# Layer norm in column halves, the key tiles earlier in the weight stream, and two query tiles split by token tile

## What is computed

```python
merged = (sigmoid(gate_fox) * (y_fox @ p_fox) + sigmoid(gate_rwkv) * (y_rwkv @ p_rwkv))
x = layer_norm(DN_ALPHA * x + merged @ w_o, ln1_g, ln1_b)
x = layer_norm(DN_ALPHA * x + peer(x, w_q, sub_keys, u_table, v_table), ln2_g, ln2_b)

def layer_norm(x, g, b):
    mu = mean(x); var = mean((x - mu) ** 2)
    return (x - mu) * rsqrt(var + 1e-5) * g + b

# peer, per token: q = x @ w_q as 8 heads x 2 halves of 128; scores against 128 keys per list;
# the top 16 of each of the 16 lists, the top 16 of their 256 sums, softmax gates,
# h = gelu(u_table[idx] @ x), output = (gate * h) @ v_table[idx]
```

## Time and profile before

| | |
|---|---|
| median of 3 runs | 1415.6 us (1414.64 to 1416.53) |
| the profiled execution, its own time | 1418.0 us |
| its span in the profile | 1416.3 us |
| TensorE busy | 1382.9 us, 98% of the span |
| VectorE, ScalarE, GpSimd busy | 892.2, 869.3, 764.5 us |
| mean granted TensorE clock | 0.994 |

### The profile page before, as it was taken

The page is one execution under the profiler, slowest core; times in us unless marked ns, Lnnn a source line. Parts: engine busy times, 40 slices in busy tenths (PEclk is TensorE's granted clock), DMA queues, the critical chain, the costliest instruction groups (busy, mean ns, idle before and its releaser), DMA issues.

```text
span 1416.3 us, 28596 instructions
## 1 busy us (share of the span) xinstructions
PE 1382.9 (98%) x9422; PEld 1220.7 (86%) x9422; DVE 892.2 (63%) x1967; ACT 869.3 (61%) x1496; POOL 764.5 (54%) x350
## 2 busy tenths in 40 slices
PE   7999999999999999999999999999999999999997
PEld 6878888887888777789999999999998888888886
DVE  3784883214753654435998049999977776655555
ACT  5475775446755656556666768888874544444443
POOL 6876889877765523877988877777750000000000
PEclk9999999999999999999999999999999999999999
DMA  6633566555443312654555556566559877666662
GB/s 199 209 124 119 193 194 194 185 185 166 147 149 122 127 53 75 208 187 155 193 178 188 180 175 201 190 201 198 200 189 329 273 243 240 208 193 191 194 193 96
DMA packets 75352, 256.63 MB, mean 181 GB/s; under 512 B 8472, under 2 KB 8856, under 8 KB 75032
## 3 DMA queue, kind: packets, MB, share of 16 engines
q1 hardware_dynamic: 64192, 231.76, 50.2%
q10 hardware_dynamic: 11096, 24.00, 4.9%
HBM read 244.72 MB, written 11.01 MB: 181 GB/s over the span
## 4 chain that ended last, share of the span: by engine, by line
PE 70%; POOL 12%; issue 8%; DVE 6%; ACT 2%; DMA 0%; POOLq 0%; ACTq 0%; DVEq 0%
PE PS L1079 60%; POOL WL L403 12%; PE PS L1124 2%; PE PS L1637 2%; PE PS L1458 1%; PE PS L1125 1%; PE PS L1416 0%; DVE GA L1804 0%; DMA fbias<-fox_bias 0%; PE PS L1363 0%; DVE H L1994 0%; DVE XS L2270 0%; DVE GA L1803 0%; DVE BK L2008 0%; PE PS L1613 0%
## 5 line engine op out<-in xcount | busy, mean ns | idle before, releaser
L403 POOL TENSOR_TENSOR WL<-RAW,WH 128x1024 fp32r<-128x1024 f32 x306 | 740.2, 2429 | 278.6 <-ACT WH L462 190.8
L1079 PE MATMUL PS<-XHL,WH 128*128 128x256 f32 x2528 | 460.8, 284 | 2.2 <-DVE XHL L1757 1.5
L953 ACT CAST WH<-RAW 128x1024 fp32r<-128x1024 f32 x252 | 263.6, 1046 | 226.5 <-PE PS L1079 211.6
L1079 PEld LDWEIGHTS PS<-XHL,WH 128*128 128x128 f32 x2528 | 394.5, 192 | 5.8 <-issue 4.0
L1079 PE MATMUL PS<-XHL,WL 128*128 128x256 f32 x1264 | 357.8, 283 | 0.0
L462 ACT CAST WH<-RAW 128x1024 fp32r<-128x1024 f32 x184 | 191.3, 1047 | 109.4 <-PE PS L1079 98.7
L1079 PEld LDWEIGHTS PS<-XHL,WL 128*128 128x128 f32 x1264 | 242.7, 192 | 0.0
L2440 DVE TENSOR_TENSOR WL<-RAW,WH 128x1024 fp32r<-128x1024 f32 x128 | 156.8, 1225 | 120.2 <-ACT WH L953 119.5
L1079 PE MATMUL PS<-WH,CH 128*128 128x512 f32 x512 | 199.2, 389 | 0.0
L1079 PE MATMUL PS<-WH,CL 128*128 128x512 f32 x512 | 199.2, 389 | 0.0
L1079 PE MATMUL PS<-WL,CH 128*128 128x512 f32 x512 | 199.2, 389 | 0.0
(11 more groups left out here) (407 smaller groups left out, 1966.4 us busy)
## 6 DMA issues: line engine op xcount, KB each, us to landing
RAW<-weights SPq DMA_DIRECT2D x438, 512.0 KB, 3.6
gates_rest<-stage ACTq DMA_DIRECT2D x32, 272.0 KB, 2.2
stage<-gates_rest ACTq DMA_DIRECT2D x32, 272.0 KB, 4.1
H<-x SPq DMA_DIRECT2D x2, 512.0 KB, 4.8
LG<-rows ACTq DMA_DIRECT2D x2, 512.0 KB, 6.3
LB<-rows ACTq DMA_DIRECT2D x2, 512.0 KB, 8.8
x<-H ACTq DMA_DIRECT2D x1, 1024.0 KB, 5.8
HY<-x ACTq DMA_DIRECT2D x1, 1024.0 KB, 13.4
```

The lines of the kernel that those rows point to most:

```text
L403: nc.gpsimd.tensor_tensor(WL[:, slot, :], RAW[:, slot, :], plain(WH[:, slot, :]), ALU.subtract).then_inc(w_lo, 1)
L953: nc.scalar.copy(WH[:, slot, :], RAW[:, slot, :]).then_inc(w_hi, 1)
L1079: last = mm(dst, a, b, start=start and k == 0, stop=stop and k == len(pairs) - 1)
```

## The change

Three edits:
1. `keys` moves in the item order from behind `w_o` to ahead of `p_rwkv`. `KK` gets another address; `fox_item(3)` counts `w_used` up by 3 in place of the keys (before, the last `w_o` item did). The places of `feed` from `p_fox` to `p_rwkv` stay as they are.
2. The layer norm works in column halves. Sums stay in PSUM; ScalarE squares each half around a pivot (twice the mean of half 0, with sign), and one-column operations of VectorE put the variance together. Half 0 of a tile is summed when its half of the product is complete (`tile_done`, `w_used`). Gain and shift are applied half by half.
3. TensorE transposes tile 0 ahead of the last `w_o` item of tile 1, multiplies `peer_q` 0 and 1 with tile 0, transposes tile 1, and multiplies the two with tile 1; `tile_low(0)` stands in VectorE's program between the two halves of tile 1. The last `v_table` items are split by halves for tile 1 alone.

```diff
-    ... ("p_fox", 4), ("p_rwkv", 4), ("w_o", 8), ("keys", 2), ("peer_q", 16), ...
+    ... ("p_fox", 4), ("keys", 2), ("p_rwkv", 4), ("w_o", 8), ("peer_q", 16), ...
-        KK = at("KK", [P, 2, 2, D], F32R, R0 + 16384)
+        KK = at("KK", [P, 2, 2, D], F32R, A0 + 40960)

 # ScalarE
-            act.wait_ge(w_used, FIRST["p_rwkv"])
+            act.wait_ge(w_used, FIRST["keys"])
...
-            feed(FIRST["w_o"] + 6)
+            feed(FIRST["w_o"] + 4)
+            def row_squares(k, t, half):
+                c = 2 * k + t
+                act.wait_ge(sem("mean_ready"), 2 * c + half + 1)
+                A(LNS[:, t, half * 512:(half + 1) * 512], PS[:, row_bank(k, t, half), :], ACT.Square,
+                  bias=row_stat(c, PIVOT), accum_out=row_stat(c, SQUARES + half)).then_inc(sem("var_ready"), 1)
+            def row_root(k, t, ms_val):
+                r = ST[:, 96 + 2 * k + t:97 + 2 * k + t]
+                act.wait_ge(sem("ms_ready"), ms_val)
+                A(r, r, ACT.Sqrt, scale=-1.0 / D ** 2).then_inc(sem("sq_ready"), 1)
+            root_table()
+            row_squares(0, 0, 0)
+            row_squares(0, 0, 1)
+            row_root(0, 0, 9)
+            feed(FIRST["w_o"] + 5)
+            feed(FIRST["w_o"] + 6)
+            tile_high(0, range(4))
+            row_squares(0, 1, 0)
+            row_squares(0, 1, 1)
+            row_root(0, 1, 10)
+            feed(FIRST["w_o"] + 7)
+            tile_high(1, range(2))
+            feed(FIRST["peer_q"])
+            tile_high(1, range(2, 4))

 # TensorE
-                last.then_inc(w_used, 1)
+                last.then_inc(w_used, 3 if c == 3 else 1)          # fox_item
             for t in range(NT):
                 for j in range(4, 8):
                     g, i = W_O_ORDER[j] // 4, W_O_ORDER[j] % 4
                     activations(T_MERGED)(2 * i + 1)
+                    if (t, j) == (1, 7):
+                        tile_transposes(0)
                     last = item_a(FIRST["w_o"] + j, i, XH, XL, 2 * g, False, i == 3, [t])
                     if t == NT - 1:
-                        last.then_inc(w_used, 1 if j < 7 else 3)
-                if t == 0:
-                    last.then_inc(sem("tile_done"), 1)
+                        last.then_inc(w_used, 1)
+                    elif j % 2:
+                        last.then_inc(sem("tile_done"), 1)
+            def query_tile(m, t):
+                ...
+                for k in range(KC):
+                    if m == 0:
+                        wait("xl_ready", KC * T_X2 + 4 * t + k // 2 + 1)
+                    mm(both[:, :, tokens], wh, XHL[:, :, k, tokens], start=(k == 0), stop=False)
+                    last = mm(both[:, 0, tokens], wl, XH[:, k, tokens], start=False, stop=(k == KC - 1))
-            for m in range(LISTS):
+            for t in range(NT):
+                if t:
+                    tile_transposes(t)
+                for m in range(2):
+                    query_tile(m, t)
+            list_scores(0)
+            for m in range(2, LISTS):
                 wait("ql_ready", m - 3)
-                item_w(FIRST["peer_q"] + m, 4 + m % 4, ready=...)
-                if m:
-                    list_scores(m - 1)
+                item_w(FIRST["peer_q"] + m, 4 + m % 4)
+                list_scores(m - 1)
 # last v_table items
-            for t in range(NT):
+            for c in range(4):
+                last = v_item(NK - 4 + c, c, stop=(c == 3), tiles=[0])
+            last.then_inc(sem("tile_done"), 2)
+            for half in range(2):
                 for c in range(4):
-                    last = v_item(NK - 4 + c, c, stop=(c == 3), tiles=[t])
+                    last = v_item(NK - 4 + c, c, stop=(c == 3), tiles=[1], halves=[half])
                 last.then_inc(sem("tile_done"), 1)

 # VectorE
+            def first_half(k, t, alpha):
+                link(V.scalar_tensor_tensor(rows, (HY if k else H)[:, t, halves[0]], alpha, rows, ALU.mult, ALU.add,
+                                            accum_out=sums))
+                V.tensor_scalar(row_stat(c, PIVOT), sums, -2.0 / D, None, ALU.mult).then_inc(sem("mean_ready"), 1)
+            def second_half(k, t, alpha, gain, shift, landed, ready, beside=None):
+                V.scalar_tensor_tensor(rows[1], H_[:, t, halves[1]], alpha, rows[1], ALU.mult, ALU.add,
+                                       accum_out=sums[1]).then_inc(sem("mean_ready"), 1)
+                wait("mean_ready", 2 * c + 2)
+                V.tensor_scalar(m, sums[0], sums[1], -1.0 / D, ALU.add, ALU.mult)
+                V.tensor_scalar(apart, sums[1], sums[0], None, ALU.subtract)
+                wait("var_ready", 2 * c + 1)
+                link(V.tensor_scalar(rest, row_stat(c, SQUARES), float(D), LN_EPS * D * D, ALU.mult, ALU.add))
+                link(V.scalar_tensor_tensor(spread, apart, apart, rest, ALU.mult, ALU.subtract))
+                wait("var_ready", 2 * c + 2)
+                V.scalar_tensor_tensor(r, row_stat(c, SQUARES + 1), -float(D), spread, ALU.mult, ALU.add).then_inc(
+                    sem("ms_ready"), 1)
+                wait("ln_landed", landed)
+                V.scalar_tensor_tensor(rows[0], rows[0], m, gain[:, halves[0]], ALU.add, ALU.mult)
+                if beside:
+                    beside()
+                wait("sq_ready", 9 + c)
+                link(V.reciprocal(r, r))
+                V.scalar_tensor_tensor(H_[:, t, halves[0]], rows[0], r, shift[:, halves[0]], ALU.mult,
+                                       ALU.add).then_inc(sem(ready), 1)
+                link(V.scalar_tensor_tensor(rows[1], rows[1], m, gain[:, halves[1]], ALU.add, ALU.mult))
+                V.scalar_tensor_tensor(H_[:, t, halves[1]], rows[1], r, shift[:, halves[1]], ALU.mult,
+                                       ALU.add).then_inc(sem(ready), 1)
             for t in range(NT):
+                alpha = ST[:, 104 + t:105 + t]
                 if t == 0:
                     wait("tile_done", 1)
                 else:
+                    used(FIRST["w_o"] + 5)
+                first_half(0, t, alpha)
+                if t == 0:
+                    wait("tile_done", 2)
+                else:
+                    tile_low(0)
                     used(FIRST["w_o"] + 7)
-                layer_norm(0, t, [t, 2 + t], ST[:, 104 + t:105 + t], LG1, LB1, 32, "x2_ready")
-            tile_low(0)
+                second_half(0, t, alpha, LG1, LB1, 32, "x2_ready")
             tile_low(1)
 # the second norm: first_half(1, 0); second_half(1, 0) with first_half(1, 1) behind its first gain pass
 # (beside); second_half(1, 1), which waits for tile_done 6
```

More of the change, by code:

```diff
@@ L61 @@
     ("qk", 8), ("v", 8), ("o", 8), ("mix_out", 8), ("w1", 32), ("w2", 32), ("ple", 2), ("ple_gate", 8),
-    ("rwkv", RW_CHUNKS), ("fox_qk", 8), ("fox_v", 4), ("gates", 16), ("p_fox", 4), ("p_rwkv", 4), ("w_o", 8),
-    ("keys", 2), ("peer_q", 16), ("u", NK), ("v_table", NK),
+    ("rwkv", RW_CHUNKS), ("fox_qk", 8), ("fox_v", 4), ("gates", 16), ("p_fox", 4), ("keys", 2), ("p_rwkv", 4),
+    ("w_o", 8), ("peer_q", 16), ("u", NK), ("v_table", NK),
 ]
@@ L337, in made, with row_bank, row_stat @@
             return PS[:, b:b + 2, :].rearrange("p b (a l j) -> p l j (b a)", a=2, l=2)[:, part_]
+        def row_bank(k, t, half):
+            return 2 * t + half if k else t + 2 * half
+        PIVOT, SQUARES, APART, REST, SPREAD = 0, 1, 3, 4, 5
+        def row_stat(c, which):
+            return ST[:, 24 + 6 * c + which:25 + 6 * c + which]
         def at_token(x, t):
@@ L1586, in _, with tile_transposes @@
                     transposes(T_MERGED, XS, "xs_ready", 5, chunks=range(4, KC))
[L1587 to L1592, removed]
-                        last.then_inc(w_used, 1 if j < 7 else 3)
-                if t == 0:
-                    last.then_inc(sem("tile_done"), 1)
-            for t in range(NT):
+            def tile_transposes(t):
                 for c in range(KC):
@@ L1686, in _, with v_item @@
             V0 = FIRST["v_table"]
-            def v_item(j, c, start=False, stop=False, tiles=range(NT)):
+            def v_item(j, c, start=False, stop=False, tiles=range(NT), halves=range(2)):
                 slot = (V0 + c) % RING
@@ L1693, in v_item @@
                     h, l = CH[:, c, t * P:(t + 1) * P], CL[c][:, t * P:(t + 1) * P]
-                    for half in range(2):
+                    for half in halves:
                         wh = WH[:, slot, half * 512:(half + 1) * 512]
@@ L2254, in _ @@
                 low_half(T_MERGED, None, range(4 * g, 4 * g + 4))
-            def layer_norm(k, t, banks, alpha, gain, shift, landed, ready):
-                H_ = HY if k else H
[L2259 to L2268, removed]
+            halves = [slice(g * 512, (g + 1) * 512) for g in range(2)]
@@ L2512 @@
         "p_fox": form_a(a["p_fox_2"][0]),
+        "keys": a["peer_sub_keys_2"][0].reshape(2, PH, NK, P).transpose(0, 3, 1, 2).reshape(2, P, D),
```

(1 more changed line is left out.)

67 lines of the change are left out of this document (38 added, 29 removed).

## The result

The changed kernel takes 1418.87 us (median of 20 runs, 1416.0 to 1422.27), the kernel before in the same sessions 1415.84 us (20 runs, 1413.45 to 1418.54): ratio 1.0022, 95% interval 1.0016 to 1.0028. The change makes the kernel slower by 3.0 us. That lies in the range on record (1413.4 to 1420.2), but 2.3 us above the forecast of 1416.6 and outside its likeliest case, which ended at 1418.4. It is just over the 0.2% that I had set as the bound of "slower", and the interval has values on both sides of that bound.

What follows compares the result with a forecast made beforehand. The prediction took TensorE, busy 98% of the span, to bound the kernel. Its terms +3.4 + 1.7 - 4.6 + 0.5 = +1.0 us, put on the median of 1415.6, gave 1416.6 us, with a range of 1413.4 to 1420.2.

Steps and rivals of the forecast that it cites:

- likeliest case: Whole kernel: the forecast itself, 1416.6 us, as a case from 1414.0 to 1418.4 us with chance 0.58.
- Part 1, the wait: Ahead of `p_rwkv`: its item 0, now fed behind the `YRH` casts, is ready later and TensorE waits, +3.4 us.
- Part 1, the clock: Behind the wait at `p_rwkv`: TensorE's clock falls, costing half of 3.4 us slow time, +1.7 us, bounds 0 and +3.3.
- the one at 402: Old trace: a TensorE hole of 2.15 us, with about half speed for 3.4 us from 402 behind it.
- Part 2: Layer norm 1 and first query tiles: query item 2 starts sooner after tile 0's `w_o` end, -4.6 us.
- I take 1.5 for the smaller matmuls: Query stage, TensorE: one tile of a split query item was counted as 1.5 us, against 1.4 from whole items.
- -5.3: Norm and queries, bound: PSUM-writing passes cost no more than known ones and TensorE's short matmuls pack as well as long.
- six passes at 0.1 more: Norm and queries, other bound: each of the six passes takes 0.1 more, gain -3.8 us.
- The 1.3 us that I put on the early transposes: End of `w_o`: tile 0's transposes ahead of the last item make it wait, delaying tile 1's norm, 1.3 us.
- The first rival: Clock falls in the query stage too, or stays low longer behind the `p_rwkv` hole: 1418.3 to 1419.9 us, chance 0.27.
- Part 3: Tail: VectorE's two norms in halves take 10.8 us for 10.27, +0.5 us, bounds +0.2 and +1.2.
- The sum: Whole kernel: wait, clock, norm with queries, and tail, +3.4 + 1.7 - 4.6 + 0.5 = +1.0 us.

Runs made afterwards that it cites:

- the keys back: Changed kernel with the key items at their old place behind `w_o`, all else of the change kept: +0.3 us against the kernel before, ratio interval 0.9990 to 1.0016.

## Why the prediction was right

**Part 1, the wait.** +3.4 forecast, +3.52 measured, at the place and with the releaser named. Feeding one item sooner took most of it away, so the reading of the feed was the cause and not a coincidence of the trace.

**Part 1, the clock.** +1.7 forecast with 0 to 3.3 as bounds; +2.62 in this trace. The mis-sized term is the slow time behind the hole, counted as 3.4 us after the one at 402; it was 5.4 us here [stretches above]. The five traces with this hole and no filling lose 1.3, 1.3, 2.2, 2.3 and 2.6 us: the mechanism is right, its size differs from execution to execution, and the mean, 1.9, is near the forecast. The time that filling the hole gave back, 1.8 us, agrees with that, if loosely. What decides between 1.3 and 2.6 in one execution stays open; I did not try it.

**Part 2.** -4.6 forecast, -4.06 measured. The step that was mis-sized is "I take 1.5 for the smaller matmuls": a tile of a query item took 1.84. Item 2 waits for the scores of list 0, and these for `QL`, which follows item 0. Rows of the changed kernel:

```profile
609.65 0.36 PE L1642 MATMUL PS<-XHL,WH 128*128 128x256 f32 x1
...
611.60 0.33 PE L1642 MATMUL PS<-XHL,WH 128*128 128x256 f32 x1
...
613.08 0.42 DVE L2382 TENSOR_TENSOR QL<-PS,QH 128x256 fp32r<-128x256 f32 x1 [0.44 <-ACT QH L907]
613.65 0.35 PE L1655 MATMUL PS<-KK,QH 128*128 128x256 f32 x1
```

Tile 1 of item 0 runs from 609.65 to 611.60 and ends 14.3 us after tile 0's end, for 13.9 in my count, where the last low parts and not the matmuls set its end. `QL` stands 1.9 us later, as counted, and the scores with their start take 0.6 for 0.42. Item 1 ends at 613.5, 16.1 us after tile 0's end for 15.4 in my count, so TensorE itself comes free hardly sooner than `QL`. The steps of VectorE were right within 0.2 us: tile 0's second half at 4.9 after tile 0's end (forecast 4.7), tile 1's at 11.9 (11.7). The bounds were not worked out: -5.3 has no sum, and six passes at 0.1 more give -4.0 and not -3.8.

The 1.3 us that I put on the early transposes was a real delay of `w_o` 7 (1.4 us), but not a price: its last matmul starts at 603.87, and VectorE comes to the half that it completes only at 604.32. Moved behind, the transposes delay tile 1's norm through the casts and low parts instead.

**The first rival** had two halves. The second fall of the clock did not come true: 1.00 throughout the query stage in the changed kernel. The other half, a longer slow time behind the hole at `p_rwkv`, came true in part, with 5.4 us for 3.4. Beside the rival stood the rule of the Trainium skill (TensorE: Matmul & The Clock Gate, Part 4: PE-mode transpose) that transposes do not count as TensorE activity the way matmuls do. By that rule the clock was to fall here; the trace of the changed kernel does not agree, with 1.00 over 607.8 to 613.5. With the keys back, where TensorE idled 0.7, 0.7 and 1.8 us around the first query tiles, the clock did fall (0.59). Whether transposes played a part in that was not isolated.

**Part 3.** +0.5 forecast, +0.94 measured, inside the bounds of 0.2 and 1.2. Two steps were counted too short, in both tiles. From the second half's sum to the first gain pass it took 1.74 us for 1.65 (0.2 together), with a wait for ScalarE's square in it that I had left out:

```profile
1404.36 0.69 DVE L2323 SCALAR_TENSOR_TENSOR PS<-HY,PS 128x512 f32<-128x512 f32 x1
...
1406.02 0.16 DVE L2332 SCALAR_TENSOR_TENSOR ST<-ST 128x1 f32<-128x1 f32 x1 [0.23 <-ACT LNS L859]
1406.10 0.75 DVE L2335 SCALAR_TENSOR_TENSOR PS<-PS,ST,LG 128x512 f32<-128x512 f32 x1
...
1408.47 0.75 DVE L2342 SCALAR_TENSOR_TENSOR PS<-PS,ST,LG 128x512 f32<-128x512 f32 x1
1409.25 0.75 DVE L2343 SCALAR_TENSOR_TENSOR HY<-PS,ST,LB 128x512 f32<-128x512 f32 x1
```

And the shift of the second half reads what the gain pass just ahead of it wrote, and starts 0.78 us behind it, for 0.7 (0.2 together).

**The sum.** +1.0 forecast, +2.9 by stretches, +3.0 by medians. Clock, query tiles and tail each came out 0.4 to 0.9 us dearer than my count, all in the same direction, and this carried the time half a microsecond past the forecast case (1414.0 to 1418.4), to where the first rival's times lie, of whose two halves only the longer slow time behind the hole happened. Three errors of one sign did not cancel, and that the sum still fell into the range is owed to its width. The main statement held: a gain of 4 us at the norm, and a loss of 6 ahead of it that belongs to the way the keys were fed.

## What to carry to other kernels

In a stream that is fed in order, moving an item ahead delays all behind it up to the next place at which the program feeds: count the items between two feeds, and look which wait the next feed stands behind. A hole of 4 us on TensorE cost it half as much again in clock (1.9 us in the mean of five traces), and so a hole is worth filling even with work that is dearer in itself (here 1.9 us more for two query items, for some 3.5 us won). Work cut by token tile loads its weights once per tile, and here that was its likely price. Cutting a pass in two to start sooner cost 0.9 us in the tail, where VectorE had no time to spare, and at the first norm no gain of it alone could be seen.

## What the runs showed of the hardware

- Matmuls of 256 and 128 columns in turn, each with its own weights, took 0.23 us a pair, where 512 and 256 took 0.345: half the columns for two thirds of the time. The weight loads started every 0.115 us without a gap.
- A 128x512 pass of VectorE that reads and writes PSUM and reads SBUF took 0.75 us, no more than the pass between SBUF tensors (0.75 us).
- VectorE's gain pass over 1024 columns of two SBUF tensors took 1.28 us alone and up to 2.2 us beside GpSimd's subtractions.
- Twelve float32 matmuls of a constant 128x128 tile (24 instructions, each with its weight load, 2.84 us, so 0.118 each) in a hole of 4.2 us kept the granted clock at 1.00.
